# Two edits to the expert stage of a two-block model step: where a block's tokens lie in the partitions, and when the two experts with a second block are computed

## The reference, cut to what matters

```python
expert_id = g_idx[:, None] * EXPERTS_PER_GROUP + top_idx          # two experts per token
def expert_block(args):
    xb, e = args                                                    # rows of one block, one expert
    act = jax.nn.silu(xb @ w_gate[e]) * (xb @ w_up[e])              # 2048 -> 256
    return act @ w_down[e]                                          # 256 -> 2048
picked = ys[slot].reshape(n, TOP_K, d)
return jnp.einsum('nkd,nk->nd', picked, weights)
x = x + gate2 * m
```

```
27 34 25 30 26 10 21 51 28 65 41 39 48 58 26 31 36 37 50 51 44 32 37 75 15 7 12 14 16 8 16 14
```

## Time and profile before

| what | value |
| --- | --- |
| median of 3 runs | 2161.09 us (2160.12 to 2162.77) |
| the profiled execution's own time | 2158.96 us |
| its span | 2157.2 us |
| PE busy | 1986.6 us, 92% of the span |
| DMA, slices 32 to 39 of 40 (1726 to 2157 us) | 363 to 408 GB/s, the last slice 164 |

### The profile page before, as it was taken

The page is one execution under the profiler, slowest core; times in us unless marked ns, Lnnn a source line. Parts: engine busy times, 40 slices in busy tenths (PEclk is TensorE's granted clock), DMA queues, the critical chain, the costliest instruction groups (busy, mean ns, idle before and its releaser), DMA issues.

```text
span 2157.2 us, 19478 instructions
## 1 busy us (share of the span) xinstructions
PE 1986.6 (92%) x7654; PEld 1019.2 (47%) x7654; DVE 817.4 (38%) x1377; ACT 313.7 (15%) x604; POOL 174.1 (8%) x190
## 2 busy tenths in 40 slices
PE   6999999999999999999999999999959987777885
PEld 3444545544444455444444445554435544444553
DVE  0375737442377355446251002522253332222222
ACT  0011111130210232100150112321210000000000
POOL 0000022000000000000000000000002211111111
PEclk9999999999999999999999999999979999999898
DMA  6575645334115443957122221143189999999994
GB/s 238 187 276 203 239 143 186 103 119 174 59 59 201 158 148 109 359 213 290 52 78 79 77 79 59 39 157 131 74 316 383 363 408 406 400 403 391 395 391 164
DMA packets 116407, 448.07 MB, mean 208 GB/s; under 512 B 20918, under 2 KB 21276, under 8 KB 77020
## 3 DMA queue, kind: packets, MB, share of 16 engines
q1 hardware_dynamic: 86460, 303.80, 36.9%
q0 software_dynamic: 24288, 118.32, 15.9%
q10 hardware_dynamic: 5568, 24.69, 3.0%
HBM read 440.39 MB, written 26.28 MB: 216 GB/s over the span
## 4 chain that ended last, share of the span: by engine, by line
PE 77%; SPq 17%; DMA 2%; issue 1%; ACT 1%; DVE 1%; ACTq 0%; POOL 0%; POOLq 0%; DVEq 0%
PE bank L974 40%; SPq L598 16%; PE bank L977 15%; PE bank L1005 6%; PE bank L1173 4%; PE bank L796 3%; PE bank L1184 2%; DMA RW<-in_w_up 1%; PE bank L842 1%; PE bank L869 1%; PE bank L1087 1%; PE bank L829 1%; DMA RH<-in_x 1%; PE bank L811 1%; PE bank L1167 0%
## 5 line engine op out<-in xcount | busy, mean ns | idle before, releaser
L974 PE MATMUL bank<-RW,RX 128*128 128x512 f32 (+1 forms) x1536 | 631.0, 567 | 5.5 <-ACT RA L1243 3.0
L974 PEld LDWEIGHTS bank<-RW,RX 128*128 128x128 f32 x1536 | 278.5, 190 | 328.7 <-issue 327.2
L977 PE MATMUL bank<-RX,RW 128*128 128x512 f32 x768 | 338.7, 594 | 1.6 <-ACT RA L1243 1.3
L1671 DVE SCALAR_TENSOR_TENSOR RG<-RG,ccol 128x2048 f32<-128x2048 f32 x90 | 212.4, 2360 | 125.2 <-DMA RG<-in_w_mod 119.8
L974 PE MATMUL bank<-RW,RM 128*128 128x512 f32 x576 | 249.9, 593 | 1.5 <-PE bank L974 1.2
L977 PEld LDWEIGHTS bank<-RX,RW 128*128 128x128 f32 x768 | 143.9, 191 | 169.1 <-issue 167.5
L974 PEld LDWEIGHTS bank<-RW,RM 128*128 128x128 f32 x576 | 108.4, 190 | 137.9 <-issue 137.1
L2384 DVE TENSOR_TENSOR RA<-RA,bank 128x128 f32<-128x128 f32 x34 | 9.8, 287 | 331.7 <-ACT RA L1633 331.6
L1243 ACT ACTIVATE RA<-bank 128x512 f32<-128x512 f32 (+3 forms) x167 | 83.1, 537 | 297.6 <-PE bank L796 82.4
L716 POOL DMA_DIRECT2D RG<-in_w_mod x96 | 51.5, 536 | 883.9 <-DVE RG L1671 534.2
L1173 PE MATMUL bank<-RW,RG 128*64 128x256 f32 x640 | 79.5, 406 | 22.2 <-DMA RW<-in_w_up 22.1
(11 more groups left out here) (258 smaller groups left out, 1625.0 us busy)
## 6 DMA issues: line engine op xcount, KB each, us to landing
RG<-in_w_mod POOLq DMA_DIRECT2D x96, 1024.0 KB, 5.3
RW<-in_w_in SPq DMA_DIRECT2D x72, 1024.0 KB, 5.0
RW<-in_w_out SPq DMA_DIRECT2D x24, 1024.0 KB, 5.2
RX<-in_w_gate SPq DMA_DIRECT2D x19, 1024.0 KB, 29.2
RX<-in_w_up SPq DMA_DIRECT2D x19, 1024.0 KB, 28.6
RW<-in_w_gate SPq DMA_DIRECT2D x19, 1024.0 KB, 29.0
RW<-in_w_up SPq DMA_DIRECT2D x19, 1024.0 KB, 28.3
RM<-in_w_down SPq DMA_DIRECT2D x18, 1024.0 KB, 30.4
```

The costliest lines, as they stand in the source:

```text
L974: ins = nc.tensor.matmul(banks[j][:, 0:width], act[:, ka, j * P:(j + 1) * P], W[:, s, kt % 4, 0:width], start=kt == 0, stop=kt == kk - 1)
L977: ins = nc.tensor.matmul(banks[j][:, :], W[:, s, kt % 4, j * P:(j + 1) * P], act[:, kt, :], start=kt == 0, stop=kt == kk - 1)
L1671: st.do(v.scalar_tensor_tensor(out=dst, in0=x, scalar=sc, in1=y, op0=op0, op1=op1), s, n)
```

## The change

It makes two edits.

First, `spot_no` takes the place of `block_no` in the comparison that puts tokens in slots. Slot s now holds the token of rank `s % 8 * 8 + s // 8`. Ranks 0 to 7 go to slots 0, 8, 16, ..., 56, ranks 8 to 15 to slots 1, 9, ..., 57, and so on: each group of eight neighbouring slots holds ranks that are 8 apart.

```diff
+TWIN_AT = (10, 18)
+        "spot_no": np.broadcast_to((np.arange(BLK) % 8 * 8 + np.arange(BLK) // 8).astype(np.float32)[None, :], (P, BLK)),
-        for pos in range(NE):
-            BLOCKS.append((pos, pos))
-            if KEPT <= pos < KEPT + TWINS:
-                BLOCKS.append((pos, NE + pos - KEPT))
+        STREAM = [e for e in range(NE) if not KEPT <= e < KEPT + TWINS]
+        for k in range(TWINS):
+            STREAM.insert(TWIN_AT[k], KEPT + k)
+        for pos, col in enumerate(STREAM):
+            BLOCKS.append((pos, col))
+            if KEPT <= col < KEPT + TWINS:
+                BLOCKS.append((pos, NE + col - KEPT))
-                    expert_at[0] = sp.value_load(permi[n // 6:n // 6 + 1, 0:1], min_val=0, max_val=NE - 1)
+                    col = STREAM[n // 6]
+                    expert_at[0] = sp.value_load(permi[col:col + 1, 0:1], min_val=0, max_val=NE - 1)
-            spot_no = C["block_no"].unsqueeze(1).unsqueeze(1).to_broadcast([P, 8, 2, BLK])
+            spot_no = C["spot_no"].unsqueeze(1).unsqueeze(1).to_broadcast([P, 8, 2, BLK])
```

## The result

The changed kernel is slower: median 2169.58 us of 6 runs (2169.27 to 2171.12) against 2161.36 us (2160.12 to 2162.77), ratio 1.004, 95% interval 1.0029 to 1.005. That is 8.2 us more; 8.7 were forecast. The profiled execution took 2169.6 us, its span is 2167.9.

What follows compares the result with a forecast made beforehand. The weight stream bounds the kernel, lasting as long as its busiest DMA engine works. Deal +11.2, first gather +1.0 and order -3.5 make +8.7 us on 2161.09: 2169.8 us, range 2162 to 2180.

Steps and rivals of the forecast that it cites:

- The map: Indirect gathers and scatters: each DMA engine serves four neighbouring partitions and the four 32 further, in each half of 64.
- the milder map: Alternative map with the second four partitions dealt in opposite order; in the tail, busiest engine some 7 us over the mean.
- The deal, +11.2: Weight stream: new slots give the busiest engine 43 more rows at 0.26 us, +11.2 us, bounds 7.3 to 15.0.
- The check that the busiest engine never rests: Weight stream: its weights and rows take 534 us against 529 available, so extra rows are paid in full.
- The order, -3.5: Expert stage near 1682 us: later twins (blocks freeing no weight buffers) close a gap, -3.5 us, bounds 0 and -4.6.
- The first gather, +1.0: Before the stream: fullest engine moves seven rows instead of four, PE waits longer, +1.0 us, bounds 0 and 2.
- The scatters: Expert stage: a fuller engine lengthens them, median landing from 9.3 to near 11 us, still covered.
- A share under 1: Sign: DMA share under 1 in 1685 to 2110 us, since odd engines run dry.
- Rival D: Twins (blocks freeing no weight buffers) at positions 10 and 18 leave engines dry: +19.2 us, 2180 us, chance 0.09.
- A: Main case: slower because the busiest engine gets more rows; 2169.8 us, range 2164 to 2178, chance 0.76.
- PE's first wait for a piece: Sign: PE waits for weights from about 1660 us on instead of 1742.
- A late step of 18.5 us: Sign: late PE steps near 18.5 us where blocks hold some 32 tokens, unchanged where they hold 36 to 58.

Runs made afterwards that it cites:

- e3: Changed kernel with rank r dealt to engine r % 8 of its half, rows nearly even over engines: 2141.2 us, 0.9915 of the kernel before.
- e5: Like e3, but every other row of eight ranks dealt in the opposite direction: 2136.7 us, 0.989 of the kernel before.
- e4: Changed kernel with ranks 0 to 7 all on a half's first engine, 8 to 15 on the second, and so on: 2190.9 us, 1.0143 of before.
- e1: Changed kernel with the old slots, so only the twins (blocks freeing no weight buffers) move, to positions 10 and 18: 2157.4 us, 0.9986 of before.
- e6: Kernel before with only the second twin (block freeing no weight buffers) moved, to position 18, the first staying at 3: 2156.9 us, 0.9986.
- e2: Changed kernel with the twins (blocks freeing no weight buffers) back at positions 3 and 4, so only the deal changes: 2171.8 us, 1.0057 of before.
- e9: Deal of e5 with the twins (blocks freeing no weight buffers) at positions 3 and 4 as before: 2142.4 us, 0.9916 of the kernel before.
- e8: Changed kernel with a scatter that writes rows instead of adding them: 2141.1 us, 0.9909 of the kernel before.

## Why the prediction was right, step by step

**The map.** Right. Eight equal engines in the tail, the e3 and e5 deals built on it that win, and the e4 deal that loses: all follow the counts. But the tail of the kernel before was no evidence for it. The prediction set 7 us, for the milder map, against the tail's 14.4, and left out what its own map gives: the busiest engine has 113 rows more than the mean (360 against 247), at 0.26 us some 29 us of mean idle time. That is as far off. It takes the packets of over 330 ns (below) to find part of the rest.

**The deal, +11.2.** Right: +12.3 alone, +11.7 as the changed kernel against e1 (1.004 - 0.9986 = 0.0054 of 2160 us), 0.27 us a row, known to about 3 us either way. Over the whole span of deals the price is lower: from e5 to e4, 252 rows more cost 0.0253 x 2160 = 54.6 us, 0.22 a row. The packet records of the kernel before agree with the lower price: an added row lasts 327 ns and overlaps the next packet by 20, a gathered one 159 and overlaps by 4, an empty packet 9 and overlaps by 3 to 4. One row more in the place of an empty packet is then (307 + 155) / 2 - 6 = 225 ns. The 0.26 counted the overlaps and the empty packets' 39 us in. At 0.225 the term is +9.7, still within what was measured.

The check that the busiest engine never rests was also weaker than "within a per cent": it found 534 us of work in 529 us, of which 3.5 were the gap. Less the overlaps the work is some 520 us, an estimate from the same records, in 525 outside the gap. The check is good to 1 or 2%, and that is 5 to 10 us, nearly the size of the term. It is the runs that show that extra rows are paid.

**The order, -3.5.** Right with the old slots: -3.0, and e6 shows that the second pause made the gap. But the prediction added it to a kernel with other slots. In e2 the heavy engines still worked there (0.45 to 0.63), so to them the gap was worth less than 3.5; over the same stretch as for e9 above, the profiled executions of e2 and the changed kernel differ by 1.3 us (536.7 and 535.4). The intervals of the times are too wide to show that.

**The first gather, +1.0.** Wrong as a mechanism. PE waited no more than 0.1 us longer for it, 9.88 us against 9.79, and in e4, whose fullest engine moves eight rows, 9.70. The stream did start 0.8 us later (1608.92 against 1608.11), but from PE's clock. These are windows of the kernel before and then of the changed one:

```profile
1604.00:1606.00 2.00, 2.00 (x14) 1.16 (x12) 1.86 (x7) 0.00 (x0) 0.00 (x0) 0.55 0.00 0
1606.00:1608.00 2.00, 2.00 (x22) 1.32 (x20) 0.71 (x4) 0.00 (x0) 0.00 (x0) 1.00 0.00 0
```

```profile
1604.00:1606.00 2.00, 2.00 (x12) 1.08 (x10) 1.86 (x7) 0.00 (x0) 0.00 (x0) 0.50 0.08 33
1606.00:1608.00 2.00, 2.00 (x14) 1.23 (x12) 0.62 (x4) 0.00 (x0) 0.00 (x0) 0.62 0.00 0
```

PE had stood idle before, the granted clock was 0.50 (1.2 of 2.4 GHz), and it came back to 1.00 about 1.7 us later than before (by the two windows' means). In e2, with the same slots, the first issue is at 1608.07, and in e1, with the old ones, at 1609.51, so this is chance of an execution and not of the change. The sum came out right to half a microsecond partly by luck: without this term it was +7.7.

**The scatters.** Their median landing rose from 9.3 to 10.3 us, not to 11, and the trace shows nothing that waited for them.

**"A share under 1".** Only just (0.99). The rate of 382 GB/s shows it better, and at the late twin it is plain: in the changed kernel the window 1774 to 1778 reads

```profile
1774.00:1778.00 4.00, 4.00 (x36) 2.20 (x34) 1.41 (x2) 0.00 (x0) 0.39 (x1) 1.00 0.49 205
```

Half the engines are dry and half are busy. Rival D feared this place; by the share, the half that decides never stopped. Rival D's sum was also off: it charged 3.5 us at each late twin and forgot that the early gap closes, so it should have been +15.7 us, 2177, inside A's range. Its time could not have told it from A; the windows do.

**Other signs.** PE's first wait for a piece after the start ends at 1670.23 us, not near 1660, against 1742.34 before. A late step of 18.5 us can't be read: between blocks that wait for weights, steps swing from 16 to 21 us in both kernels.

**Open.** e3 and e5 win less than rows times 0.22 to 0.27 from e1 (15 us for 87 rows, 21 for 108: 0.18 and 0.19). A limit shared by the engines is not it: the commonest record of a weight packet is 309 ns in all these kernels, and the mean of those under 330 ns is 311 in each. That the slowest of sixteen nearly equal engines is later than the one or two busiest of before is a guess that no run tests.

## What to carry to other kernels

A transfer over all partitions is done when its slowest DMA engine is, so count the work per engine, not in total, and count it in time: here an added row of 4 KB took longer than a weight packet of 8 KB. Look at the DMA share at the end of a long stream: the slide over 20 us at 0.4 to 0.1 was here unequal load that had been there all along. Deal the rows of an indirect DMA by the groups of partitions that one engine serves. A block that frees no buffers belongs where the backlog of loads is long, not next to another such block at the start, and not at the end, where the engine that lags cannot catch up.

The Trainium skill ("DMA: Bandwidth & Descriptors", The descriptor swizzle) has the formula for the groups; e3 to e5 are its test for indirect gathers and scatters, and they agree with it: 273, 504 and 252 rows on the busiest engine gave 2141.2, 2190.9 and 2136.7 us.

## What was not expected of the hardware

A row that is added to memory takes its engine 327 ns for 4 KB, twice the 159 ns of a row only gathered and more than the 309 ns of an 8 KB weight packet. It is the addition and not the direction: in e8, where half of the rows are still scattered, a 4 KB row lasts 162 ns in the mean. Taking the addition out won 28 us, as much as the even deal of e3. And starvation seems not to show as idle time alone: in 1685 to 2110 us, 540 of the changed kernel's 18154 packets of 8 KB lasted over 330 ns (218 us in all over 309 each), 279 of 19028 in the kernel before (104 us), 728 of 17738 in e4 and 25 of 19297 in e3. The count follows the inequality of the engines. That the long packets are those of engines that had run dry is argued from this, not shown.
